# Another order of the weight units around a linear recurrence, without GpSimd's low halves there

## The reference, cut to what matters

```python
def recurrent_block(x, w_in, conv_w, conv_b, w_gate, b_gate, lam, w_out):
    u = x @ w_in                                  # 1024 x 2048
    gate, rec = u[..., :D_RNN], u[..., D_RNN:]
    rec = causal_depthwise_conv(rec, conv_w, conv_b)
    h = rg_lru(rec, w_gate, b_gate, lam)
    return (jax.nn.gelu(gate) * h) @ w_out

def rg_lru(x, w_gate, b_gate, lam):               # 8 blocks of 128
    g = einsum('bsnd,nde->bsne', xb, w_gate) + b_gate
    r, i = sigmoid(g[..., :128]), sigmoid(g[..., 128:])
    a = exp(-8 * r * softplus(-lam))
    b = sqrt(-expm1(2 * log_a)) * (i * x)
    ...                                           # h[t] = a[t] * h[t-1] + b[t]

# second block
kv_me = rmsnorm_2(mem, norm_mem[l]) @ w_mem_kv[l]  # keys and values of the memory
```

## Time and profile before

| | us |
|---|---|
| runs | 1111.03, 1111.36, 1114.2 |
| median | 1111.36 |
| span of the profiled execution | 1109.1 |
| TensorE busy | 1044.4 |
| VectorE (DVE) busy | 656.4 |
| ScalarE (ACT) busy | 568.8 |
| GpSimd (POOL) busy | 112.8 |

### The profile page before, as it was taken

How to read it: one execution, slowest core, us unless ns; L and a number is a source line. 1 busy time by engine, 2 the same in 40 slices (tenths; PEclk the granted TensorE clock), 3 DMA queues, 4 the chain that set the end, 5 groups by cost and what they waited for, 6 DMA issues and landing times. The chain is left out here.

```text
span 1109.1 us, 16405 instructions
## 1 busy us (share of the span) xinstructions
PE 1044.4 (94%) x6694; PEld 933.3 (84%) x6694; DVE 656.4 (59%) x887; ACT 568.8 (51%) x854; POOL 112.8 (10%) x117
## 2 busy tenths in 40 slices
PE   5987999999989989989999989999999979999997
PEld 5986789989978866679999979988899869999996
DVE  5658665555556665465555555455654748776674
ACT  6576454444454554554444445355645347656552
POOL 3535200000000011320000000000000610000000
PEclk9999999999999988999999999999999999999999
DMA  9543565555535531176555546543334535556520
GB/s 318 187 151 126 178 237 184 189 186 189 189 114 196 183 114 39 44 234 196 178 190 185 188 149 185 185 127 113 115 114 151 192 114 190 190 168 211 189 79 38
DMA packets 117971, 180.41 MB, mean 163 GB/s; under 512 B 3113, under 2 KB 93577, under 8 KB 117913
## 3 DMA queue, kind: packets, MB, share of 16 engines
q1 hardware_dynamic: 116099, 174.16, 47.3%
q0 software_dynamic: 1696, 5.39, 1.4%
q10 hardware_dynamic: 118, 0.05, 0.0%
HBM read 178.48 MB, written 1.10 MB: 162 GB/s over the span
## 5 line engine op out<-in xcount | busy, mean ns | idle before, releaser
L942 PE MATMUL PS<-XA,whi 128*128 128x256 f32 x2640 | 487.6, 286 | 9.2 <-DVE XA L1340 6.8
L1319 DVE TENSOR_TENSOR wlo<-raw,whi 128x2048 fp32r<-128x2048 f32 x153 | 352.4, 2308 | 178.2 <-ACT whi L577 173.8
L942 PEld LDWEIGHTS PS<-XA,whi 128*128 128x128 f32 x2640 | 418.1, 194 | 21.1 <-issue 15.6
L577 ACT ACTIVATE whi<-raw 128x2048 fp32r<-128x2048 f32 x158 | 301.7, 1913 | 159.2 <-PE PS L961 129.1
L942 PE MATMUL PS<-XA,wlo 128*128 128x256 f32 x1320 | 375.8, 285 | 0.0
L942 PEld LDWEIGHTS PS<-XA,wlo 128*128 128x128 f32 x1320 | 255.5, 194 | 0.0
L961 PE MATMUL PS<-whi,XB 128*128 128x512 f32 x800 | 226.0, 390 | 1.0 <-DVE XB L1551 1.0
L961 PEld LDWEIGHTS PS<-whi,XB 128*128 128x128 f32 x800 | 147.6, 188 | 30.1 <-issue 1.7
L961 PE MATMUL PS<-wlo,XB 128*128 128x512 f32 x400 | 127.4, 390 | 0.0
L961 PE MATMUL PS<-whi,XA 128*128 128x512 f32 x272 | 79.7, 404 | 12.2 <-DVE XA L1420 8.4
L961 PEld LDWEIGHTS PS<-wlo,XB 128*128 128x128 f32 x400 | 75.1, 188 | 15.9
(11 more groups left out here) (185 smaller groups left out, 957.5 us busy)
## 6 DMA issues: line engine op xcount, KB each, us to landing
raw<-in_w_up SPq DMA_DIRECT2D x32, 1024.0 KB, 5.4
raw<-in_w_down SPq DMA_DIRECT2D x32, 1024.0 KB, 4.9
raw<-in_w_ffn_up SPq DMA_DIRECT2D x22, 1024.0 KB, 5.1
raw<-in_w_in SPq DMA_DIRECT2D x21, 1024.0 KB, 5.2
raw<-in_w_ffn_down SPq DMA_DIRECT2D x11, 1024.0 KB, 4.9
raw<-in_a_w_in SPq DMA_DIRECT2D x8, 1024.0 KB, 8.3
raw<-in_w_kv SPq DMA_DIRECT2D x8, 1024.0 KB, 5.2
raw<-in_w_mem_kv SPq DMA_DIRECT2D x4, 1024.0 KB, 5.3
```

Source lines behind the costliest of these rows:

```text
L577: act.activation(whi[:, s, :], raw[:, s, :], ACT.Copy).then_inc(s_hi, 1)
L942: ins = pe.matmul(PS[:, bank_of(g), 0:T], w[:, k, P * m:P * m + P], X[:, k0 + k, part, :], start=(i == 0 and part == 0 and w is hi), stop= ...
L1319: dve.tensor_tensor(wlo[:, s, :], raw[:, s, :], whi[:, s, :].bitcast(F32), ALU.subtract).then_inc(s_lo, 1)
```

## The change

The recurrent half's four units come first, then one gate unit, the recurrence's own gates, and the other three gate units. In TensorE's program the second gate unit stands between the recurrence's gates and the memory's transposes, the third and fourth between the transposes and the memory's keys. Gate groups are evacuated as plain copies (`gate_out`), and one GELU for each half of the channels follows when all four gate units are evacuated. ACT's decay steps stand right behind the sigmoids, each ahead of or behind a split; the scales, scans and splits of DVE are interleaved anew, the two gate products are put behind both scans, and DVE makes the low halves of units 12 to 15 itself.

```diff
--- before.py
+++ after.py
@@ -28,7 +28,7 @@
 UNIT = 2048
 
 
-U_REC, U_GATE, U_LRU = [0, 1, 3, 5], [2, 4, 6, 7], 8
+U_REC, U_GATE, U_LRU = [0, 1, 2, 3], [4, 6, 7, 8], 5
 U_MEMK, U_MEMV, U_ROUT = 9, 11, 13
 U_MLP0 = 17
 U_K, U_Q, U_V, U_O = 49, 53, 57, 61
@@ -44,7 +44,7 @@
 FFN_STEPS = FFN // 256
 
 
-G_REC, G_GATE, G_MEMK = [0, 2, 6, 10], [4, 8, 12, 14], 16
+G_REC, G_GATE, G_MEMK = [0, 2, 4, 6], [8, 10, 12, 14], 16
 G_MLP0, G_MLP1 = 20, 52
 G_QMB, G_KMB, G_QSW, G_KSW, G_QME = 84, 88, 92, 96, 97
 G_G2 = [101, 109, 125]
@@ -136,8 +136,7 @@
     w_mem = A["w_mem_kv_2"][0]
     rec = [cols(a_in, KT, D + 256 * i) for i in range(4)]
     gate_ = [cols(a_in, KT, 256 * i) for i in range(4)]
-    w_units += [rec[0], rec[1], gate_[0], rec[2], gate_[1], rec[3], gate_[2]]
-    w_units += [gate_[3], A["a_w_gate"][0].rearrange("k p n -> p k n")]
+    w_units += rec + [gate_[0], A["a_w_gate"][0].rearrange("k p n -> p k n")] + gate_[1:]
     w_units += [cols(w_mem, KT, 256 * i) for i in range(2)]
     w_units += [rows(w_mem, 512 * i, 4, 512, 512) for i in range(2)]
     w_units += [rows(A["a_w_out"][0], 256 * i) for i in range(4)]
@@ -363,7 +362,6 @@
 
         SPLIT_AT = {5: U_O, 9: U_O + 1, 13: U_O + 2}
 
-        POOL_SPLIT_MEM = [u + LEAD for u in range(U_MEMK, U_MEMV + 2)]
         POOL_SPLIT_O = [u + LEAD for u in (U_V + 3, U_O, U_O + 1, U_O + 2)]
 
         def pieces(bank0=4):
@@ -506,8 +504,6 @@
                 pool.wait_ge(s_lru, 4 * h + 4)
                 v = ig[:, 4 * h:4 * h + 4, :]
                 pool.tensor_tensor(v, v, xc[:, 4 * h:4 * h + 4, :], ALU.mult).then_inc(s_ix, 1)
-            for u in POOL_SPLIT_MEM:
-                split(u)
             pool.wait_ge(s_ew, 32)
             roots(SQ_NORM[2])
 
@@ -653,24 +649,33 @@
                     act.wait_ge(s_convd, k + 1)
                     act.activation(XB[:, k, 0, :], xc[:, k, :], ACT.Copy).then_inc(s_ch, 1)
 
-            def gate_unit(i):
-                unit_a(U_GATE[i], G_GATE[i], [gate[:, 2 * i + m, :] for m in range(2)], ACT.Gelu_apprx_tanh)
+            def gate_out(i):
+
+                for m in range(2):
+                    evac(G_GATE[i] + m, BEFORE(U_GATE[i]) + m + 1, gate[:, 2 * i + m, :])
+
+            def decay(h):
+
+                act.wait_ge(s_lru, 8)
+                act.wait_ge(s_cc, 1)
+                for n in range(4 * h, 4 * h + 4):
+                    act.activation(av[:, n, :], rg[:, n, :], ACT.Exp, scale=cneg[:, n:n + 1]).then_inc(s_a, 1)
+                for n in range(4 * h, 4 * h + 4):
+                    act.activation(rg[:, n, :], rg[:, n, :], ACT.Tanh, scale=cpos[:, n:n + 1]).then_inc(s_a, 1)
 
             rec_unit(0)
             rec_unit(1)
             conv_hi(0)
 
             act.wait_ge(s_ew, 32)
-            gate_unit(0)
+            rec_unit(2)
             conv_hi(1)
-            rec_unit(2)
-            gate_unit(1)
+            rec_unit(3)
             conv_hi(2)
             squares(SQ_NORM[1], xn, lambda i: act.wait_ge(s_mem, 16))
-            rec_unit(3)
-            gate_unit(2)
+            split(U_GATE[0] + LEAD)
             conv_hi(3)
-            gate_unit(3)
+            gate_out(0)
             for n in range(8):
 
                 act.wait_ge(s_step, BEFORE(U_LRU) + n + 1)
@@ -679,22 +684,26 @@
                                          bias=vecs[:, R_BG + 2 * n + e:R_BG + 2 * n + e + 1])
                 ins.then_inc(s_lru, 1)
             split(U_LRU + LEAD)
+            decay(0)
+            split(U_GATE[1] + LEAD)
+            gate_out(1)
+            decay(1)
             norm_hi(1, [(XB, R_MEM)], bank=4)
-            split(U_MEMK + LEAD)
-            act.wait_ge(s_lru, 8)
-            act.wait_ge(s_cc, 1)
-            for h in range(2):
-
-                for n in range(4 * h, 4 * h + 4):
-                    act.activation(av[:, n, :], rg[:, n, :], ACT.Exp, scale=cneg[:, n:n + 1]).then_inc(s_a, 1)
-                for n in range(4 * h, 4 * h + 4):
-                    act.activation(rg[:, n, :], rg[:, n, :], ACT.Tanh, scale=cpos[:, n:n + 1]).then_inc(s_a, 1)
-                for m in range(2):
-                    evac(G_MEMK + 2 * h + m, BEFORE(U_MEMK + h) + m + 1, kT_me[:, 2 * h + m, :])
+            split(U_GATE[2] + LEAD)
+            gate_out(2)
             for h in range(2):
                 act.wait_ge(s_q, h + 1)
                 act.activation(rg[:, 4 * h:4 * h + 4, :], rg[:, 4 * h:4 * h + 4, :], ACT.Sqrt).then_inc(s_sq, 1)
-            split(U_MEMK + 1 + LEAD)
+            split(U_GATE[3] + LEAD)
+            gate_out(3)
+            for h in range(2):
+                v = gate[:, 4 * h:4 * h + 4, :]
+                act.wait_ge(s_evac, G_GATE[2 * h + 1] + 2)
+                act.activation(v, v, ACT.Gelu_apprx_tanh).then_inc(s_gelu, 1)
+            for h in range(2):
+                split(U_MEMK + h + LEAD)
+                for m in range(2):
+                    evac(G_MEMK + 2 * h + m, BEFORE(U_MEMK + h) + m + 1, kT_me[:, 2 * h + m, :])
             split(U_MEMV + LEAD)
             for k in range(2):
                 act.wait_ge(s_y, k + 1)
@@ -1010,12 +1019,9 @@
 
             pe.wait_ge(s_tables, 16 * 4)
             pe.matmul(PS[0:16, 7, 0:384], relb[0:32, :], onehot[0:32, :], start=True, stop=True).then_inc(s_eps, 1)
-            unit_a(U_REC[1], G_REC[1])
-            for i in range(2):
-                unit_a(U_GATE[i], G_GATE[i])
-                unit_a(U_REC[2 + i], G_REC[2 + i])
-            unit_a(U_GATE[2], G_GATE[2])
-            unit_a(U_GATE[3], G_GATE[3])
+            for i in range(1, 4):
+                unit_a(U_REC[i], G_REC[i])
+            unit_a(U_GATE[0], G_GATE[0])
             have(U_LRU)
             s = U_LRU % SLOTS
             for n in range(8):
@@ -1030,8 +1036,11 @@
                     pe.matmul(dst, w, XB[:, n, 1, :], start=False, stop=False, skip_group_check=True)
                     ins = pe.matmul(dst, wl, XB[:, n, 0, :], start=False, stop=(e == 1), skip_group_check=True)
                 ins.then_inc(s_step, 1)
+            unit_a(U_GATE[1], G_GATE[1])
             pe.wait_ge(s_lru, 8)
             norm_T(1, bank=4)
+            unit_a(U_GATE[2], G_GATE[2])
+            unit_a(U_GATE[3], G_GATE[3])
             for i in range(2):
                 unit_a(U_MEMK + i, G_MEMK + 2 * i, X=XB, xready=NORM_HI[1] if i == 0 else None)
             for i in range(2):
@@ -1307,7 +1316,7 @@
                     return
                 s = u % SLOTS
                 dve.wait_ge(s_hi, it * units + u + 1)
-                if u - 1 in POOL_SPLIT_MEM + POOL_SPLIT_O:
+                if u - 1 in POOL_SPLIT_O:
 
                     dve.wait_ge(s_lo, u)
                 if u in U_SWQ:
@@ -1392,23 +1401,17 @@
                     if w < 2:
                         link(ins)
 
-            split(U_REC[0] + LEAD)
-            conv(0)
-            split(U_REC[1] + LEAD)
-            conv(1)
-            for i in range(2):
-                split(U_GATE[i] + LEAD)
-                split(U_REC[2 + i] + LEAD)
-                conv(2 + i)
+            for i in range(4):
+                split(U_REC[i] + LEAD)
+                conv(i)
             norm(1, xn, [])
-            split(U_GATE[2] + LEAD)
-            split(U_GATE[3] + LEAD)
+            split(U_GATE[0] + LEAD)
+            split(U_LRU + LEAD)
 
             def half(v, h):
                 return v[:, 4 * h:4 * h + 4, :].rearrange("p a b -> p (a b)")
 
-            norm_lo(1, [(XB, R_MEM)], bank=4, late=U_LRU + LEAD)
-            for h in range(2):
+            def scale2(h):
 
                 dve.wait_ge(s_a, 8 * h + 4)
                 link(dve.tensor_tensor(half(sq, h), half(av, h), half(av, h), ALU.mult))
@@ -1420,21 +1423,37 @@
                 dve.tensor_tensor(XA[:, 4 * k:4 * k + 4, 1, :], xc[:, 4 * k:4 * k + 4, :],
                                   XA[:, 4 * k:4 * k + 4, 0, :].bitcast(F32), ALU.subtract).then_inc(s_yl, 1)
 
-
-            dve.wait_ge(s_evac, G_GATE[3] + 2)
-            for h in range(2):
+            def scan(h):
+
                 dve.wait_ge(s_sq, h + 1)
                 dve.wait_ge(s_ix, h + 1)
                 link(dve.tensor_tensor(half(ig, h), half(ig, h), half(rg, h), ALU.mult))
-                if h == 1:
-                    y_lo(0)
                 for k in range(4 * h, 4 * h + 4):
                     ins = dve.tensor_tensor_scan(rg[:, k, :], av[:, k, :], ig[:, k, :], 0.0, ALU.mult, ALU.add)
                 link(ins)
+
+            def y_out(h):
+                dve.wait_ge(s_gelu, h + 1)
                 dve.tensor_tensor(half(xc, h), half(rg, h), half(gate, h), ALU.mult).then_inc(s_y, 1)
+
+            scale2(0)
+            split(U_GATE[1] + LEAD)
+            scale2(1)
+            norm_lo(1, [(XB, R_MEM)], bank=4, late=U_GATE[2] + LEAD)
+            scan(0)
+            split(U_GATE[3] + LEAD)
+            scan(1)
+            dve.wait_ge(s_step, AFTER[U_GATE[3]])
+            for h in range(2):
+                y_out(h)
+            split(U_MEMK + LEAD)
```

(4 more changed lines are left out.)

## The result

| | median us | runs | ratio to the kernel before |
|---|---|---|---|
| before | 1114.17 | 1111.03 to 1116.25, 7 runs | |
| changed | 1104.91 | 1104.06 to 1110.12, 7 runs | 0.9932 (0.9916 to 0.9948) |

The change makes the kernel faster by 0.68%, 7.6 us of 1114 with an interval of 5.8 to 9.4. The plain difference of the two medians is 9.3 us; the text goes by the ratio. The profiled execution has a span of 1103.5 us against 1109.1.

The account below looks back on a forecast made before the run. TensorE, busy 94%, was taken as the bound, so only gaps in its queue count. Keys at 80.7 plus 44.7 gave 125.4 instead of 136.1: 10.7 us off, 1098.4 of span, plus 2.3 to the median, 1100.7 us; range 1096.5 to 1107.5.

Parts of the forecast that it names:

- GpSimd's low halves made DVE late: Recurrence's scans and products: DVE operations meeting GpSimd's low halves run long, an excess of 10.9 us on a chain.
- The rival of DVE being slow by its place: Scans and products slow by place in the recurrence: 1111 us with one half slow (0.04), 1121.9 with both (0.04).
- Four splits on DVE for 9.2 us, hidden: Four splits of 2.31 us move from GpSimd to DVE, 9.2 us, placed where TensorE need not wait.
- an end after 98: Sign of being wrong: DVE's split for the second value unit, forecast to end at 97.3, needed at 97.9, ends after 98.
- The first gap, 1.0 us and 1.7 of clock: TensorE near 42 us: gate unit starts 1.0 us earlier after a 1.4 us gap, and 1.7 us of low clock goes.
- A new gap of 4.5 us with low clock: Recurrence's gates near 52 us: TensorE waits 4.5 us for the first sigmoid; low clock costs 1.7 on TensorE, 0.7 on ACT.
- Keys at 80.7, set by both queues: Start of the memory's keys: TensorE's queue reaches it at 80.7 us and ACT's at 80.6, so the two meet.
- From the keys to the end 44.7 us without a wait: Memory's keys to end of output product: 44.7 us if TensorE never waits, ending at 125.4 instead of 136.1.
- The clock staying low for longer: Rival: low clock after the new gap lasts up to the second gate unit, end at 128 to 129, 1104 us; chance 0.18.
- Table loads: Rival: four table changes on ACT's queue between 53 and 88 us cost 1.4 us more each, 1106 us; chance 0.03.
- The key norm's table load, hidden: Key norm's roots at 365 us: a new table load of 1.28 us under 2.1 us of cover, so costing nothing.
- Given back later: Rival: the table load at 365 us on the path, or the clock falling in later gaps, 1106 us; chance 0.09.

Follow-up runs that it names:

- the kernel with the filled gap: Changed kernel with TensorE's second gate unit put between the fourth and fifth block of the recurrence's gates: 0.9939 of the kernel before (0.9918 to 0.9960).
- the second profile: Profile of the changed kernel run once more, unaltered: 0.9935 of the kernel before (0.9915 to 0.9955).

## Why the prediction was right, and where it was off

The forecast was faster by 10.7 us with a range of 1096.5 to 1107.5 us; 7.6 us and 1104.91 were measured. Of the 4.2 us between 1100.7 and 1104.91, 2.8 are the base: the median of before was 1111.36 in the three runs shown and 1114.17 in seven. The other 1.4 are the size of the gain. In the profiles the stretch became 9.5 and 8.7 us shorter, 1.2 and 2.0 less than the forecast: the keys came 1.3 and 2.1 us later than forecast, and 0.2 came back behind them. What lies between these and the 7.6 us of the ratio, 1 to 2 us, no trace places; the spread of the clock behind the stretch is larger.

- *GpSimd's low halves made DVE late.* Right, and shown: old order without them 2.44 us for the scans, new order with them 6.83 for the second scans and 10.91 for the outputs. The rival of DVE being slow by its place fell with the same two kernels.
- *Four splits on DVE for 9.2 us, hidden.* Right: each takes 2.28 or 2.29 us, and no wait of TensorE from the keys on is for a low half. The slack of 0.6 us at the second value unit shrank to 0.4: its low half ends at 98.80, TensorE's first matmul of it is at about 99.2. The prediction had named an end after 98 as a sign of being wrong. The end did come later, but only because the keys and all behind them had moved by 1.3 us; the wait that the sign stood for did not appear.
- *The first gap, 1.0 us and 1.7 of clock.* Size off: it was 1.9 us in one profile and 2.2 in the other, not 1.4, and the clock fell in the first. TensorE was through with the fourth unit at 41.6 us, not 42.0, and ACT resumed at 40.8, not 40.6; the gate unit started at 43.55, close to the 43.4 of the sum. It did not matter, since this time is taken up by the wait for the sigmoids; that I counted it as a saving at all was a mistake of the sum's parts, not of its end, which went by the two queues.
- *A new gap of 4.5 us with low clock.* Right: 3.8 and 5.3 us, and 3.4 to 5.8 us at 0.50 behind it.
- *Keys at 80.7, set by both queues.* The term that was mis-sized. They started at 82.0 and 82.8. In the first profile 1.0 us of the 1.3 is there at the first sigmoid (56.70, not 55.7) and 0.3 comes behind it. Convolutions beside GpSimd's low halves take 3.67 and 3.69 us; the kernel before has one with GpSimd idle:

```profile
49.13 2.71 DVE L1387 SCALAR_TENSOR_TENSOR arena<-arena,vecs 128x256 f32<-128x256 f32 x6
```

This puts 0.23 and 0.72 us of idling on ACT, where I had 0.6 for one. ACT also resumed 0.16 us later, and its operations take 0.5 us more than my rounded terms. The sum had both queues at the keys at once; in fact ACT set the pace, as the kernel with the filled gap shows, and TensorE had 0.7 us of room in the first profile and 0.5 in the second.
- *From the keys to the end 44.7 us without a wait.* 44.5 measured.
- *The clock staying low for longer.* It did in the second profile (5.80 us at 0.50, last sigmoid 0.8 us later), at the price of 0.8 us of the end; the rival had 3.
- *Table loads.* No ACT load costs more than its row: 55.41 to 56.70 is 1.29 us. The 2.66 us of the Trainium skill (ScalarE: Activation LUTs, What ACT_TABLE_LOAD costs) with its drain are not what this trace shows, and that rival fell.
- *The key norm's table load, hidden.* Right. It stands in front of the root, and TensorE's transposes, which answer to the earlier trace rows, waited for nothing:

```profile
353.59 1.28 ACT L762 ACT_TABLE_LOAD   x1
354.89 0.23 ACT L762 ACTIVATE rstd<-ss 128x32 f32<-128x32 f32 x1
```

- *Given back later.* The mechanism named, the clock in later gaps, took 3.9 us of the profiled execution and 0.1 of the second. That is a spread between executions of one kernel; no fixed cost of the change is seen.

What the sum did not say is that the order's part is almost nothing by itself (0.9997), and at most 2 to 3 us beside the removal.

## What to carry to other kernels

A helper engine's operation costs what it blocks: GpSimd's four low halves relieved DVE of 9.2 us, and took up to 10.9 us back on the chain that set the end. Look for operations of one shape with two durations in the timeline, and lay the other engine's operations beside them. Before filling a gap of the busiest engine, follow whose queue ends the next wait; a gap that another engine's queue dictates only moves, and here it moved to a place where, with the low clock behind it, the product ended 1.2 to 2.0 us later. And a wait should stand in front of the first instruction that needs it: moving one gave 4.8 to 5.6 us of the stretch and 6.5 to 7 by the medians, nearly as much as the change.

## What the runs showed of the hardware

A DVE operation with two SBUF operands waits for GpSimd operations that read SBUF, and not for memsets: four scans of 0.6 us took 8.97 us beside additions of 2.55 us, and 2.44 beside eight memsets. Beside these additions, and beside GpSimd's low halves of weights, one DVE operation got in for each of GpSimd's, a scan of 0.6 us as well as a product of 1.2, so that many short ones lost more than a few long ones. This is no fixed rule: elsewhere a DVE step of 0.48 us got in between none of six GpSimd operations and took 4.88.

The granted clock fell behind a gap of 1.9 us in one execution (0.56) and stayed up behind one of 2.2 us of the same kernel in another (1.00). Gap length alone does not tell; over 970 us of identical work the clock made 3.8 us between these two executions (976.24 and 972.44).
